# Opening of a two-block transformer kernel: norm and the first three weight tiles' products slice by slice, eight of sixteen modulation dots as wide products

## What is computed

```python
c_act = jax.nn.silu(c)
mod = (c_act @ w_ada[l] + b_ada[l])[:, None, :]        # 9 vectors of 1,024
sh0, sc0, g0, sh1, sc1, g1, sh2, sc2, g2 = jnp.split(mod, 9, axis=-1)
h = _rmsnorm(x, norm_g[l, 0]) * (1.0 + sc0) + sh0      # x * rsqrt(mean(x*x) + eps) * g
x = x + 0.5 * g0 * _swiglu(h, ffn_w_gate[l, 0], ffn_w_up[l, 0], ffn_w_down[l, 0])
```

## Time and profile before

| | us |
|---|---|
| median of 3 runs | 3693.24 (3690.15 to 3695.98) |
| the profiled execution | 3690.65 |
| its span, first to last instruction | 3688.9 |

### The profile page before, as it was taken

One profiled execution on the slowest core, in us unless ns is written; L12 is line 12 of the kernel. 1 busy time (PEld: TensorE's weight loads), 2 busy tenths in 40 slices (PEclk: granted clock), 3 DMA queues, 4 the chain that ended last, 5 costly groups with the idle time before them and its releaser, 6 DMA issues. The chain is left out here.

```text
span 3688.9 us, 42867 instructions
## 1 busy us (share of the span) xinstructions
PE 3412.1 (92%) x14072; PEld 2357.5 (64%) x14072; DVE 2136.9 (58%) x4134; ACT 1320.3 (36%) x2721; POOL 1702.1 (46%) x1088
## 2 busy tenths in 40 slices
PE   8999999999999999999999999999878777877877
PEld 6888876788888888866888876755433333333332
DVE  5645557443326546566333046788878768767664
ACT  3332326443324332245433233444333233223322
POOL 2545532444455546423544533455545544444552
PEclk9999999999999999999999999999989998998999
DMA  6536430133445445300233331399999999999999
GB/s 250 190 114 239 155 103 2 47 98 95 158 142 188 159 160 211 138 29 13 91 97 97 103 98 46 140 409 421 421 412 422 422 422 421 422 422 414 422 422 378
DMA packets 140782, 829.41 MB, mean 225 GB/s; under 512 B 15704, under 2 KB 16864, under 8 KB 64352
## 3 DMA queue, kind: packets, MB, share of 16 engines
q0 software_dynamic: 73728, 536.90, 35.0%
q1 hardware_dynamic: 66912, 290.73, 22.9%
HBM read 825.48 MB, written 2.10 MB: 224 GB/s over the span
## 5 line engine op out<-in xcount | busy, mean ns | idle before, releaser
L282 POOL TENSOR_TENSOR wlo<-wraw,whi 128x1024 fp32r<-128x1024 f32 x344 | 872.8, 2542 | 1099.7 <-ACT whi L278 1099.5
L278 ACT ACTIVATE whi<-wraw 128x1024 fp32r<-128x1024 f32 x344 | 363.6, 1058 | 657.6 <-DMA wraw<-in_wts 385.4
L289 PE MATMUL f_ps<-f_hh,whi 128*128 128x512 f32 x1344 | 522.8, 389 | 0.0
L290 PE MATMUL f_ps<-f_hl,whi 128*128 128x512 f32 x1344 | 522.8, 389 | 0.0
L291 PE MATMUL f_ps<-f_hh,wlo 128*128 128x512 f32 x1344 | 522.8, 389 | 0.0
L598 DVE TENSOR_TENSOR f_a<-f_sg,f_ps 128x512 f32<-128x512 f32 x88 | 60.5, 688 | 504.7 <-PE f_ps L291 489.8
L2228 POOL DMA_INDIRECT g_own<-in_uv,idx x185 | 221.6, 1198 | 202.6 <-PE g_psF L2350 115.5
L2397 ACT ACTIVATE g_dotb<-g_dotb 128x4 f32<-128x4 f32 (+2 forms) x164 | 33.5, 204 | 773.3 <-DVE g_dotb L2640 645.2
L2228 POOL DMA_INDIRECT g_low<-in_uv,idx x151 | 180.2, 1194 | 266.3 <-PE g_psF L2350 222.5
L2350 PE MATMUL g_psF<-g_low,g_diagb 128*128 128x512 f32 x400 | 217.3, 674 | 80.1 <-ACT g_diagb L2409 80.1
L291 PEld LDWEIGHTS f_ps<-f_hh,wlo 128*128 128x128 f32 x1344 | 252.3, 188 | 52.7
(11 more groups left out here) (554 smaller groups left out, 6970.8 us busy)
## 6 DMA issues: line engine op xcount, KB each, us to landing
wraw<-in_wts SPq DMA_DIRECT2D x354, 512.0 KB, 3.5
m_wrow<-in_ada SPq DMA_DIRECT2D x44, 1024.0 KB, 7.5
m_erow<-in_ada SPq DMA_DIRECT2D x28, 1024.0 KB, 5.3
p_wt<-in_wtok SPq DMA_DIRECT2D x2, 3168.0 KB, 10.0
p_wt<-in_w SPq DMA_DIRECT2D x2, 3072.0 KB, 9.6
g_own<-in_uv,idx POOLq DMA_INDIRECT x185, 26.3
g_low<-in_uv,idx POOLq DMA_INDIRECT x151, 23.3
xT<-in_xT SPq DMA_DIRECT2D x2, 1024.0 KB, 17.9
```

The lines of the kernel that those rows point to most:

```text
L278: self.nc.scalar.activation(self.T.whi[:, j % 4], self.T.wraw[:, j % 2], ACT.Copy).then_inc(self.M["w_hi"], 1)
L282: self.nc.gpsimd.tensor_tensor(self.T.wlo[:, j % 4], self.T.wraw[:, j % 2], self.T.whi[:, j % 4].bitcast(F32), ALU.subtract).then_inc(self ...
L289: self.nc.tensor.matmul(out, hi, xh, start=first, stop=False)
L290: self.nc.tensor.matmul(out, hi, xl, start=False, stop=False)
```

## The change

`first_modulation` is gone. `ffn` of layer 0 now begins (flag `begun`) with a block `first_products`, which does the following.

- Eight of the 16 dots, those of the shift, become two rows of 512 results (`dots(g, q)`): TensorE multiplies the silu of `c` as a column (128x1 stationary, fp32) with 128x512 of the modulation weights, eight such products per group `g`. ScalarE copies the row from PSUM (`flat_line`), four small products turn it into four columns (`turn`), and VectorE adds the bias (`moved`). The other eight dots, those of the gain, stay on VectorE.
- The norm sums: `total(k)` multiplies a 128x128 matrix of ones (over 1,024) with the 128x512 square, so the sum stands in all partitions at once. Square root and reciprocal are over 128x512, in SBUF; `spread` is gone.
- The norm, the gain, the split and the products of three weight tiles (`trio`, nine products a slice) go slice by slice. `trio(0)` to `trio(3)` alternate with the four pieces of group 1 of the wide products; `turn(1)` stands ahead of `trio(4)`. Tile 3 is multiplied in the next block, by `times(0, 3)`.
- ScalarE rounds four tiles: three behind the root, the fourth behind `high(5)`. GpSimd makes their remainders. SyncE loads two more tiles (those of unit 1's start) as the raw buffers come free, so that the stage ends with six tiles loaded.
- In the `ffn` block the first unit is taken out of the loops, counts are raised for what is done already, and unit 1's rounding begins in this block.

The diff, with the removed function and the blank lines cut; the hunks that are left out allocate buffers, and set `begun`.

```diff
@@ -153,91 +153,229 @@
-def first_modulation(nc, T):
...
+TRIO = 3
+GROUP = 4
+def first_products(nc, T, wrow, own, hh, hl, u, prod, ps, psD, psE):
+    third, fourth, sq, line = own
+    M = T.sems.take(nc, "first", "lc_c lc_col lc_silu lc_const lc_x*2 lc_par lc_rest m_wide*8 m_row*8 m_dot m_ch m_bg m_line m_flat "
+                            "m_turn m_shift n_sq n_sum n_root n_rstd n_u n_hi n_lo w_in*6 w_hi w_lo")
+    raws = [T.wraw[:, 0], T.wraw[:, 1], third[:, :], fourth[:, :]]
+    shift, gain, above = T.mod[:, 0:8], T.gain[:, 0:8], T.mod[:, 8:16]
+    wide = [wrow[:, 4 * g:4 * g + 4].rearrange("p a d -> p (a d)").rearrange("p (c n) -> p c n", c=KD) for g in range(2)]
+    turned = (ps[:, TRIO], psD[:, 0])
+    root = T.rstd
+    with nc.Block() as block:
+        @block.sync
+        def _(sp):
+            def group(g, q):
+                sp.dma_start(wide[g][:, 2 * q:2 * q + 2], T.d["adaw"][g, :, 2 * q:2 * q + 2]).then_inc(M["m_wide"][4 * g + q], 16)
+            def row(k):
+                sp.dma_start(wrow[:, 8 + k], T.d["ada"][0, 4 + k // 2][:, k % 2]).then_inc(M["m_row"][k], 16)
+            def weights(n):
+                sp.dma_start(raws[n], T.d["wts"][n]).then_inc(M["w_in"][n], 16)
+            def x(a):
+                sp.dma_start(T.xT[:, 4 * a:4 * a + 4], T.d["xT"][:, 4 * a:4 * a + 4]).then_inc(M["lc_x"][a], 16)
+            sp.dma_start(T.ccol[:, :], T.d["ccol"]).then_inc(M["lc_col"], 16)
+            for q in range(2):
+                group(0, q)
+            sp.dma_start(T.crow[:, :], T.d["c"]).then_inc(M["lc_c"], 16)
+            sp.dma_start(T.const[:, :], T.d["const"]).then_inc(M["lc_const"], 16)
+            x(0)
+            for q in range(2, 4):
+                group(0, q)
+            row(0)
+            x(1)
+            sp.dma_start(T.par[:, 0:P_LNG], T.d["par"][0][:, 0:P_LNG]).then_inc(M["lc_par"], 16)
+            row(1)
+            for n in range(TRIO):
+                weights(n)
+            row(2)
+            row(3)
+            for q in range(4):
+                group(1, q)
+            row(4)
+            row(5)
+            weights(3)
+            row(6)
+            row(7)
+            for n in (4, 5):
+                sp.wait_ge(M["w_lo"], n - 3)
+                sp.dma_start(T.wraw[:, n - 4], T.d["wts"][n]).then_inc(M["w_in"][n], 16)
+            sp.dma_start(T.par[:, P_LNG:], T.d["par"][0][:, P_LNG:]).then_inc(M["lc_rest"], 16)
+            sp.dma_start(T.q1[:, :], T.d["q1"]).then_inc(M["lc_rest"], 16)
...
+        @block.scalar
+        def _(act):
+            act.wait_ge(M["lc_col"], 16)
+            nc.scalar.activation(T.ccol[:, :], T.ccol[:, :], ACT.Silu).then_inc(M["lc_silu"], 1)
+            act.wait_ge(M["lc_c"], 16)
+            nc.scalar.activation(T.crow[:, :], T.crow[:, :], ACT.Silu).then_inc(M["lc_silu"], 1)
+            def square(k):
+                act.wait_ge(M["lc_x"][k // 4], 16)
+                if k >= 2:
+                    act.wait_ge(M["n_sum"], k - 1)
+                nc.scalar.activation(sq[:, k % 2], T.xT[:, k], ACT.Square).then_inc(M["n_sq"], 1)
+            def flat_line(g):
+                act.wait_ge(M["m_line"], g + 1)
+                nc.scalar.activation(line[0:1, g], psD[0:1, g], ACT.Copy).then_inc(M["m_flat"], 1)
+            def round_weights(n):
+                act.wait_ge(M["w_in"][n], 16)
+                nc.scalar.activation(T.whi[:, n], raws[n], ACT.Copy).then_inc(M["w_hi"], 1)
+            def high(k):
+                act.wait_ge(M["m_shift"], k // GROUP + 1)
+                act.wait_ge(M["n_u"], k + 1)
+                nc.scalar.activation(hh[:, k], u[:, k % 2], ACT.Identity, bias=shift[:, k:k + 1]).then_inc(M["n_hi"], 1)
+            for k in range(4):
+                square(k)
+            flat_line(0)
+            for k in range(4, KD):
+                square(k)
+            act.wait_ge(M["n_sum"], KD)
+            act.wait_ge(M["m_ch"], 3)
+            nc.scalar.activation(root[:, :], T.psN[:, :], ACT.Sqrt, bias=T.eps[:, 0:1]).then_inc(M["n_root"], 1)
+            for n in range(TRIO):
+                round_weights(n)
+            for k in range(4):
+                high(k)
+            flat_line(1)
+            high(4)
+            high(5)
+            round_weights(3)
+            high(6)
+            high(7)
+        @block.gpsimd
+        def _(pool):
+            for n in range(TRIO + 1):
+                pool.wait_ge(M["w_hi"], n + 1)
+                nc.gpsimd.tensor_tensor(T.wlo[:, n], raws[n], T.whi[:, n].bitcast(F32), ALU.subtract).then_inc(M["w_lo"], 1)
+        @block.tensor
+        def _(pe):
+            def dots(g, q):
+                pe.wait_ge(M["m_wide"][4 * g + q], 16)
+                for c in (2 * q, 2 * q + 1):
+                    mm = nc.tensor.matmul(psD[0:1, g], T.ccol[:, c:c + 1], wide[g][:, c], start=c == 0, stop=c == KD - 1)
+                if q == 3:
+                    mm.then_inc(M["m_line"], 1)
+            def turn(g):
+                pe.wait_ge(M["m_flat"], g + 1)
+                for k in range(GROUP):
+                    mm = nc.tensor.matmul(turned[g][:, k:k + 1], line[0:1, g, k * P:(k + 1) * P], T.const[0:1, C_IDENT:C_IDENT + 1],
+                                          start=True, stop=True, skip_group_check=True)
+                mm.then_inc(M["m_turn"], 1)
+            def total(k):
+                pe.wait_ge(M["n_sq"], k + 1)
+                nc.tensor.matmul(T.psN[:, :], T.const[:, C_ONES:C_ONES + P], sq[:, k % 2], start=k == 0,
+                                 stop=k == KD - 1).then_inc(M["n_sum"], 1)
+            def trio(k):
+                w = slice(k * P, (k + 1) * P)
+                pe.wait_ge(M["n_hi"], k + 1)
+                for j in range(TRIO):
+                    nc.tensor.matmul(ps[:, j], T.whi[:, j, w], hh[:, k], start=k == 0, stop=False)
+                    nc.tensor.matmul(ps[:, j], T.wlo[:, j, w], hh[:, k], start=False, stop=False)
+                pe.wait_ge(M["n_lo"], k + 1)
+                for j in range(TRIO):
+                    nc.tensor.matmul(ps[:, j], T.whi[:, j, w], hl[:, k], start=False, stop=k == KD - 1)
+            pe.wait_ge(M["lc_silu"], 1)
+            for q in range(2):
+                dots(0, q)
+            pe.wait_ge(M["lc_const"], 16)
+            for k in range(4):
+                total(k)
+            for q in range(2, 4):
+                dots(0, q)
+            keep_busy(nc, T, pe, psE, 2)
+            turn(0)
+            keep_busy(nc, T, pe, psE, 2)
+            for k in range(4, KD):
+                total(k)
+            keep_busy(nc, T, pe, psE, 8)
+            pe.wait_ge(M["w_lo"], TRIO)
+            for k in range(KD):
+                if k < 4:
+                    trio(k)
+                    dots(1, k)
+                else:
+                    if k == 4:
+                        turn(1)
+                    trio(k)
+        @block.vector
+        def _(dve):
...
+            dve.wait_ge(M["lc_silu"], 2)
+            dve.sem_inc(M["m_dot"], 1)
+            def dot(k):
+                dve.wait_ge(M["m_row"][k], 16)
+                mod_dot(nc, T, dve, M, wrow[:, 8 + k], prod, T.raw[:, KD + k:KD + k + 1], k)
+            def moved(g):
+                c = slice(GROUP * g, GROUP * g + GROUP)
+                dve.wait_ge(M["m_turn"], g + 1)
+                nc.vector.tensor_tensor(shift[:, c], turned[g][:, 0:GROUP], T.par[:, P_BADA + GROUP * g:P_BADA + GROUP * g + GROUP],
+                                        ALU.add).then_inc(M["m_shift"], 1)
+            def scaled(k):
+                dve.wait_ge(M["m_dot"], k + 2)
+                link(nc.vector.scalar_tensor_tensor(gain[:, k:k + 1], T.raw[:, KD + k:KD + k + 1], T.par[:, P_NG + k:P_NG + k + 1],
+                                                    above[:, k:k + 1], ALU.mult, ALU.add))
+                if k >= 2:
+                    dve.wait_ge(M["n_lo"], k - 1)
+                nc.vector.scalar_tensor_tensor(u[:, k % 2], T.xT[:, k], gain[:, k:k + 1], root[:, :], ALU.mult,
+                                               ALU.mult).then_inc(M["n_u"], 1)
+            def low(k):
+                dve.wait_ge(M["n_hi"], k + 1)
+                nc.vector.scalar_tensor_tensor(hl[:, k], u[:, k % 2], shift[:, k:k + 1], hh[:, k].bitcast(F32), ALU.add,
+                                               ALU.subtract).then_inc(M["n_lo"], 1)
+            dot(0)
+            dve.wait_ge(M["lc_par"], 16)
+            nc.vector.scalar_tensor_tensor(above, T.par[:, P_BADA + 8:P_BADA + 16], 1.0, T.par[:, P_NG:P_NG + 8], ALU.add,
+                                           ALU.mult).then_inc(M["m_bg"], 1)
+            dve.wait_ge(M["m_bg"], 1)
+            moved(0)
+            dot(1)
+            dve.wait_ge(M["n_root"], 1)
+            nc.vector.reciprocal(root[:, :], root[:, :]).then_inc(M["n_rstd"], 1)
+            dve.wait_ge(M["n_rstd"], 1)
+            scaled(0)
+            scaled(1)
+            low(0)
+            for k in range(2, KD):
+                dot(k)
```

(60 more changed lines are left out.)

100 lines of the change are left out of this document (14 added, 86 removed).

## The result

| | before | after |
|---|---|---|
| median, us | 3691.02 (3690.15 to 3695.98, 5 runs) | 3706.16 (3705.23 to 3713.01, 5 runs) |
| span of the profiled execution, us | 3688.9 | 3703.7 |
| unit 1 starts, us from the span's start | 68.07 | 81.05 |
| first stage border (VectorE's first `y`) | 411.80 | 424.69 |

The changed kernel is slower: the ratio is 1.0044, with a 95% interval of 1.0029 to 1.0058, or 11 to 21 us on 3691. The forecast was slower, 3705.2, 12.0 above a median of 3693.24 of three runs. That the two times lie only 1.0 apart is partly luck: the median of before is 2.2 lower with five runs, and the difference is 15.1. Unit 1 starts 12.98 later, where the prediction had 12.0, and the stage border lies 12.89 later. So the opening is the cause of most of it, and its loss is carried on to that border.

A forecast was written before the change was run, and what follows sets the result against it. TensorE bounds the kernel, so unit 1's start decides: earlier trio -7.6, opening tiles +18.2, border +0.6 and late weights +0.8 give +12.0 on the median 3693.24, so 3705.2 us; range 3698 to 3711.

The forecast's parts named there:

- hinge: Behind slice 3: the second shift line is copied, turned and moved before `trio(4)`; from 55.6 to 59.7 us.
- rival (b): Wide products in slices and norm cost 0.22 us each instead of 0.86; +4.2, 3697.4; chance 0.08.
- slices 15.0: First four slices: nine products and two wide ones each, 15.0 us together before any clock loss.
- The fourth remainder's price of 2.2: Last four slices: GpSimd's fourth-tile remainder meets `scaled(6)` on VectorE; 2.2 us, bounds 0 and 2.2.
- Rival (a): Opening without late table load (1.28), contention (1.1, 2.2), lower clock (2.0) or wait for clears (0.8): +4.6, 3697.8; chance 0.10.
- 1.28 on the path: Before the root: sqrt's table load comes behind the wait for the last sum, adding 1.28 us.
- 1.1 on GpSimd: Before the trio: VectorE's `scaled` slips between two remainders and delays GpSimd by 1.1 us.
- 4 x 3.76: First four slices: 3.76 us each, nine products at 2.04 together and two wide ones at 1.72.
- The lower clock: First slices: after TensorE's 4.8 us idle, four us at half speed lose 2.0 us (bounds 0 and 4).
- later tiles are well ahead: Next block, after unit 1's first tile: later weights are ready in time, remainders 2.4 us each against products 5.44.
- (c): Norm stage: one-column weights don't hold the clock up; totals and wide products take up to 7 us more; +19, 3712; chance 0.10.
- (d): Opening: early start wins, TensorE limiting throughout; +0.5 without hinge, -1.9 with start at 36.1, -9.7 with cheap wide products; chance 0.02.

The follow-up runs named there:

- the repeat: The changed kernel run once more, unchanged; trio at 39.08 us, unit 1 at 79.47 in place of 81.05.
- the first experiment: Changed kernel with group 1's wide products and turn ahead of the trio, in place of fillers; unit 1 at 69.28, ratio to the kernel before 1.0003.
- the second: Changed kernel with the fourth tile's remainder moved from GpSimd to VectorE, behind `low(7)`; unit 1 starts 2.07 us earlier than with the same clock.
- the last kernel: Changed kernel, all repairs, plus reciprocal ahead of `dot(2)` and gains, unit 2's loads ahead of second `erow` load; unit 1 at 59.65, ratio to before 0.9983.
- the run by tokens: Changed kernel with norm sums by token, root and reciprocal over 128x4, `spread` into PSUM, six fillers for eight; unit 1 at 80.95.
- the one before it: Changed kernel with repairs combined: early rounding, early sqrt, group 1 before slice 1, remainder on VectorE, counts before clears; unit 1 at 63.53, ratio to before 0.9988.

## Why the prediction was right

The sign and the size were right (+12.0 at unit 1 against +12.98, or +11.4 in the repeat), and the mechanism of the large terms is the one that was named. Several small terms were wrong and cancelled. Step by step:

| step | predicted | measured |
|---|---|---|
| sums end | 27.0 | 28.8 |
| table load on the path | 1.28 | 0 to 0.3 |
| reciprocal starts | 29.0 | 29.81 |
| trio starts | 38.5 | 39.27 |
| first four slices | 17.1 | 17.8 |
| hinge (copy, turn, `moved`, u, high) | 4.1 | 3.7 |
| last four slices | 13.5 | 13.2 |
| border and tile 3 to unit 1 | 6.9 | 7.1 |
| unit 1 | 80.1 | 81.05 |

**Held.** The wide product costs what its moving columns cost (3.59 for four at a time, 0.90 each), though its weight load is one column (0.08 to 0.09): rival (b) is out. Group 1 among the slices and the hinge behind it were put in the terms "slices 15.0" and "57.7 to 59.7"; the first experiment gives them back. The fourth remainder's price of 2.2 is 2.1 by the second. The Trainium skill, page SBUF — State Buffer, section "Who interferes with whom", says that a VectorE instruction with two SBUF inputs contends with a GpSimd one that reads SBUF, and that issue order decides who blocks. The trace agrees: 2.28, 2.79 and 2.38 beside GpSimd, 0.22 and 0.75 without it. Rival (a), no surcharges at all, is out with it, though two of its five, the table load and in the repeat the lower clock, did stay away.

**Failed, "1.28 on the path".** The count of waits, two, was to put the load behind the wait for the last sum. It came ahead of that wait too, right behind the last square, and was hidden. The sums ending 1.8 late made up for it: 1.1 of that is the first x half, at 12.36 in place of 11.2, and the rest is TensorE's products, each step a little longer than counted. These errors cancel to 0.8, which is luck. Why the load came ahead of the wait here is not shown.

**Failed, "1.1 on GpSimd".** GpSimd ran at its usual 2.34 each and was done at 37.76. The whole delay fell on VectorE: (2.28 + 2.79) - (0.21 + 0.75) = 4.1, of which 1.5 shows at the trio's start, since the trio could not have begun before 37.8.

**Mis-sized, "4 x 3.76".** A slice took 4.07. Its nine products take 2.26 and not 2.04, about 0.1 more at each change between them and the wide ones (the last kernel, with no wide product among its later slices, shows 2.04), and the two wide ones take 1.81 and not 1.72.

**The lower clock, "2.0".** It was 1.4 in after (5.50 for the first slice against 4.07) and 0 in the repeat. The prediction treated as certain what depends on the execution. It missed the same fall at 60 to 66, which VectorE's pitch hid: with the clock up there (more fillers) unit 1 was no earlier.

**Failed, "later tiles are well ahead".** Unit 2 waited 1.54. The step reckoned with remainders and products alone, and left out that the loads of unit 2 stand in SyncE's queue behind an `erow` load that waits for VectorE's dots, one of them 3.43 beside GpSimd. It did not show at the border because before's own end of stage lost 1.4, which is luck too.

**Rivals (c) and (d).** The clock stayed up through the norm in after, so (c) is out there; that products with one moving column lower it is suggested by before and the run by tokens, and not shown, as the clock once fell with ones as well. (d), the early start, failed in this form for the reason given, VectorE and the hinge. In the last kernel, where both are out of the way and more is changed besides, the start at 35.75 does win.

What stays open is which part of the span's difference (14.8) beyond 12.9 belongs to the change. The rest, 1.9, lies in stages of unchanged code that differ by more than that between executions (below).

## What to carry to other kernels

Work that fills gaps has to go where the gap is: here TensorE multiplied fillers, products whose results nobody uses, for 7 us and then did the same amount of useful work in the middle of the path. In a queue that runs in order, look at what stands behind a wait, and at what a "free" instruction ahead of the critical one may meet of GpSimd's work; the last kernel differs from the one before it only in such places. Take two limits away together, or the first repair seems worth little.

## What the runs showed of the hardware that was not expected

The granted clock behind an idle time of 3.45 is not the same in each execution: the same kernel ran at 0.50 and at 1.00 from 39 to 42. The attention stage, code that no kernel here touches, shows it too. Windows of before, and of after:

```profile
559.80:685.70 125.90, 121.37 (x1044) 82.36 (x1044) 91.08 (x257) 77.59 (x250) 38.46 (x64) 0.97 0.01 1
1616.40:1739.40 123.00, 118.48 (x1044) 80.35 (x1044) 90.89 (x257) 77.55 (x251) 38.44 (x64) 1.00 0.01 1
```

```profile
572.70:695.70 123.00, 118.50 (x1044) 80.40 (x1044) 90.99 (x257) 77.49 (x251) 38.21 (x64) 1.00 0.01 1
1624.90:1752.40 127.50, 122.83 (x1044) 83.59 (x1044) 91.27 (x257) 77.56 (x251) 38.21 (x64) 0.96 0.01 2
```

The same 1,044 products take 123.0 to 127.5 with a mean clock of 1.00 to 0.96, and which of the two layers is the slow one changes. Single times of one kernel lie several us apart (3683 to 3699 for before, 17 runs), of which such stretches are a part, and so the opening was read from timestamps. A scalar_tensor_tensor over one column (0.21 alone) is caught beside GpSimd like one over 512, and its own size does not set the price: in six cases, of 0.86, 1.61, 2.17, 2.28, 2.38 and 2.39, it ended within 0.02 of the end of the GpSimd instruction beside it. So the price is what is left of that instruction, at most about a whole remainder, and not a constant. The other engine pays where it comes second: with a dot of 2.93 on VectorE since 27.38, GpSimd's remainder at 29.27 took 3.25.
